# A decoder step on one core: expert turns of the second half reassigned between four stages, and the first weight blocks of three stages loaded one stage ahead

## The reference

```python
n1 = rms_norm(x, norm1_w) * (1 + sc1) + sh1
h = n1 @ w_in                                    # 8704 columns
oa = hgrn(h) ; ob = merge of 3 window attentions # softmax-weighted by head
mix = sigmoid(gA) * (oa @ w_branch_a) + sigmoid(gB) * (ob @ w_branch_b)
x = x + g1 * (mix @ w_out)
n2 = rms_norm(x, norm2_w) * (1 + sc2) + sh2
q = rms_norm((n2 @ wq).reshape(T, 8, 256), qn_w)
s1, s2 = q[..., :128] @ k1, q[..., 128:] @ k2    # top 16 of each, then 16 of 256 pairs
x = x + g2 * sum over 8 heads x 16 picks of  softmax(sc) * gelu(n2 . u[e]) * v[e]
```

## The kernel before

| stage of the second half | before | after |
|---|---|---|
| norm 1, project, hgrn | 130 | 130 |
| attention | 26 | 27 |
| merge | 34 | 14 |
| branch | 4 | 7 |
| out | 4 | 8 |
| norm 2 | 6 | 6 |
| query | 14 | 26 |
| rest (alone) | from 242 | from 242 |

## Time and profile before

### The profile page before, as it was taken

One profiled execution on the slowest core, in us unless ns is written; L12 is line 12 of the kernel. 1 busy time (PEld: TensorE's weight loads), 2 busy tenths in 40 slices (PEclk: granted clock), 3 DMA queues, 4 the chain that ended last, 5 costly groups with the idle time before them and its releaser, 6 DMA issues. The chain is left out here.

```text
span 4682.4 us, 46850 instructions
## 1 busy us (share of the span) xinstructions
PE 3284.7 (70%) x14275; PEld 1729.4 (37%) x14275; DVE 2604.3 (56%) x6546; ACT 1943.4 (42%) x6689; POOL 1482.3 (32%) x1167
## 2 busy tenths in 40 slices
PE   4998878764997899776664478796555555555556
PEld 2777665641543335444442145472111111111111
DVE  2171532366545565386556643536767767667674
ACT  1122330145445644464543321434545545545554
POOL 2553100253322223222223210213444444444443
PEclk7998789887998999876887789897777777777779
DMA  5534244388988889876898995758999999999998
GB/s 207 214 131 147 67 134 146 122 322 341 383 329 299 304 322 382 311 265 239 342 351 341 419 363 184 255 192 325 425 413 426 426 411 421 420 407 422 420 414 340
DMA packets 311887, 1449.31 MB, mean 310 GB/s; under 512 B 41042, under 2 KB 102386, under 8 KB 163283
## 3 DMA queue, kind: packets, MB, share of 16 engines
q0 software_dynamic: 152064, 1107.36, 58.8%
q1 hardware_dynamic: 145202, 331.75, 20.2%
q10 hardware_dynamic: 14368, 7.21, 0.5%
HBM read 1378.82 MB, written 74.57 MB: 310 GB/s over the span
## 5 line engine op out<-in xcount | busy, mean ns | idle before, releaser
L2408 POOL DMA_INDIRECT uv_ring<-in_peer_uv,pick_idx x1024 | 1169.3, 1142 | 2394.8 <-PE expert_acc L2573 1999.5
L2573 PE MATMUL expert_acc<-uv_ring,diag 128*64 128x512 f32 x3968 | 1281.5, 782 | 738.7 <-ACT diag L2543 708.0
L2500 DVE SCALAR_TENSOR_TENSOR uv_ring<-uv_ring,n_pairs 128x1024 f32<-128x1024 f32 x1024 | 1245.2, 1231 | 690.2 <-DMA uv_ring<-in_peer_uv,pick_idx 609.7
L2573 PEld LDWEIGHTS expert_acc<-uv_ring,diag 128*64 128x64 f32 x3968 | 294.9, 165 | 1622.6 <-ACT diag L2543 1112.5
L2530 ACT ACTIVATE gelu_cube<-dots_now 128x2 f32<-128x2 f32 x528 | 106.0, 201 | 947.8 <-DVE uv_ring L2500 916.8
L2538 ACT ACTIVATE pick_weight<-gelu_tanh,pick_share 128x1 f32<-128x1 f32 x1056 | 350.9, 379 | 17.7
L2543 ACT ACTIVATE diag<-half_pattern,pick_weight 128x64 f32<-128x64 f32 x1024 | 300.4, 340 | 16.5
L692 PE MATMUL h_acc_q<-in_w_all_q,n_all_q 128*128 128x512 f32 x640 | 288.3, 604 | 0.0
L2533 ACT ACTIVATE gelu_tanh<-gelu_cube,dots_now 128x1 f32<-128x1 f32 x1056 | 253.2, 286 | 16.2
L2535 ACT ACTIVATE pick_share<-dots_now,pick_prob 128x1 f32<-128x1 f32 x1056 | 245.2, 279 | 0.0
L689 PE MATMUL h_acc_q<-n_all_q,in_w_all_q 128*128 128x272 f32 x896 | 219.2, 401 | 10.1 <-DMA in_w_all_q<-in_w_in 10.1
(11 more groups left out here) (440 smaller groups left out, 4830.8 us busy)
## 6 DMA issues: line engine op xcount, KB each, us to landing
in_w_p<-in_w_in SPq DMA_DIRECT2D x34, 1024.0 KB, 7.2
in_w_all_q<-in_w_in SPq DMA_DIRECT2D x17, 2048.0 KB
ada_w<-in_w_ada SPq DMA_DIRECT2D x12, 2048.0 KB, 8.0
uv_ring<-in_peer_uv,pick_idx POOLq DMA_INDIRECT x1024, 14.7
past_keys_q<-in_past_keys SPq DMA_DIRECT2D x16, 1024.0 KB, 10.1
past_rows_q<-in_past_values SPq DMA_DIRECT2D x16, 1024.0 KB, 10.3
score_pair<-scores SPq DMA_DIRECT2D x66, 128.0 KB, 7.0
wq_raw_p<-in_peer_wq SPq DMA_DIRECT2D x16, 512.0 KB
```

Of the source, the lines that this page charges most:

```text
L2408: pool.indirect_dma_start(self.rows_of(part, s), None, self.x["peer_uv"][0], bass.IndirectOffsetOnAxis(ap=self.idx[:, q % 2, s, k:k + 1], ...
L2500: ins = dve.scalar_tensor_tensor(out=row, in0=row, scalar=1.0, in1=self.n2[:, tile % 2, s if tile < LAST_TILE else 0, :], op0=ALU.mult, op ...
L2573: ins = pe.matmul(self.acc[s * 64:(s + 1) * 64, c, :], self.diag[:, part % DIAGS, s, :], rows, start=first, stop=last)
```

## The change

The COST values are raised in branch, out and query of the second half and lowered in merge, `FRONT_US` goes from 2010 to 2003, and the turns move as the table above says. The tiles and semaphores of the first weight blocks become objects (`BranchWeights`, `OutWeights`, `PeerWeights`) that are allocated a stage earlier, and their `first()` is issued by SP in the stage in front: branch blocks 0 and 1 at the start of merge in the first half (in the second half still in branch, but ahead of the gates), out blocks 0 and 1 (1 MB each) in branch after its first loads in both halves, and query's keys, key weights and blocks 0 and 1 in norm 2 in both halves. Later blocks are loaded as before.

```diff
+class BranchWeights:
+    def load(self, m):
+        for j, name in enumerate(("w_branch_a", "w_branch_b")):
+            self.nc.sync.dma_start(self.w[:, m % 2, j], self.x[name][m]).then_inc(self.landed[m % 2], 16)
+    def first(self):
+        self.load(0)
+        self.load(1)
...
+class OutWeights:
+    def load(self, q):
+        self.nc.sync.dma_start(self.w[:, q % 2], self.w_out[q]).then_inc(self.landed[q % 2], 16)
...
+class PeerWeights:
+    def first(self):
+        self.load_keys(0)
+        with self.nc.allow_non_contiguous_dma("a weight for each column"):
+            self.nc.sync.dma_start(self.key_w[:], self.x["peer_qn_w"].rearrange("a (j p) -> p (a j)", p=P)).then_inc(self.key_w_in, 16)
+        self.load(0)
+        self.load(1)
...
 def norm_phase(...):
+        if peer_weights is not None:
+            peer_weights.first()
         for n, w, at in tiles:
...
 def merge_phase(...):
-    COST, COST_S = 12.0, 40.0
+    COST, COST_S = 5.2, 17.0
...
+        if branch_weights is not None:
+            branch_weights.first()
         beside.gap("sp", 2)
...
 def branch_phase(...):
-    COST = 2 * HEADS * 2 * sum(max(0.11, k * 0.00042) for _, k in pieces)
+    COST = 3.6 * HEADS * 2 * sum(max(0.11, k * 0.00042) for _, k in pieces)
...
-            at_least(sp, y_done, 2 * (m - 1))
-            for j, name in enumerate(("w_branch_a", "w_branch_b")):
-                sp.dma_start(w[:, s, j], x[name][m]).then_inc(w_in[s], 16)
+            if m > 1:
+                sp.wait_ge(y_done, 2 * (m - 1))
+                weights.load(m)
...
+        if span.samples:
+            weights.first()
         load(0)
         load(1)
+        out_weights.first()
...
 def out_phase(...):
-    COST = DC * 2 * max(0.11, PART * 0.00042)
+    COST = DC * 3.6 * max(0.11, PART * 0.00042)
...
-        load(0)
         for n, w, at in tiles:
             sp.dma_start(x1[0:w, n, :], src_rows(at, w)).then_inc(rows_in, 16)
...
-        load(1)
         next_gains.load()
...
 def query_phase(...):
-    C_Q = (3 if span.split else 3.7) * DC * sum(max(0.11, k * 0.00046) for _, k in pieces)
-    C_S = 0.8
+    C_Q = (3 if span.split else 7.0) * DC * sum(max(0.11, k * 0.00046) for _, k in pieces)
+    C_S = 1.5
...
-            if u < UNITS:
+            if 1 < u < UNITS:
...
-        load_w(0)
-        if span.split:
-            load_w(1)
-        load_keys(0)
-        with nc.allow_non_contiguous_dma("a weight for each column"):
-            sp.dma_start(key_w[:], x["peer_qn_w"].rearrange("a (j p) -> p (a j)", p=P)).then_inc(key_w_in, 16)
...
-FRONT_US = 2010.0
+FRONT_US = 2003.0
```

More of the change, by code:

```diff
@@ new lines, with __init__, load, load_keys @@
+class OutWeights:
+    def __init__(self, nc, keep, tag, x):
+        self.nc, self.w_out = nc, x["w_out"]
+        self.w = keep("w_out" + tag, [P, 2, DC, 2 * P])
+        self.landed = [nc.alloc_semaphore(name="w_out0_in" + tag), nc.alloc_semaphore(name="w_out1_in" + tag)]
+    def load(self, q):
[4 more added lines that the diff above has]
+class PeerWeights:
+    def __init__(self, nc, keep, tag, x):
+        self.nc, self.x = nc, x
+        self.raw, self.keys, self.key_w = keep("wq_raw" + tag, [P, 2, DC, P]), keep("peer_keys" + tag, [P, 2, 2, P]), keep("peer_key_w" + tag, [P, 2])
+        sem = lambda name: nc.alloc_semaphore(name=name + tag)
+        self.raw_in, self.keys_in, self.key_w_in = [sem("wq0_in"), sem("wq1_in")], [sem("peer_keys0_in"), sem("peer_keys1_in")], sem("peer_key_w_in")
+    def load(self, u):
+        self.nc.sync.dma_start(self.raw[:, u % 2], self.x["peer_wq"][u]).then_inc(self.raw_in[u % 2], 16)
+    def load_keys(self, h):
+        for j, name in enumerate(("peer_k1", "peer_k2")):
+            self.nc.sync.dma_start(self.keys[:, h % 2, j, :], self.x[name][0, h]).then_inc(self.keys_in[h % 2], 16)
+    def first(self):
+        self.load_keys(0)
+        with self.nc.allow_non_contiguous_dma("a weight for each column"):
+            self.nc.sync.dma_start(self.key_w[:], self.x["peer_qn_w"].rearrange("a (j p) -> p (a j)", p=P)).then_inc(self.key_w_in, 16)
+        self.load(0)
+        self.load(1)
@@ L280, in norm_phase @@
+def norm_phase(nc, ph, span, beside, const, gains, loaded_here, n_hi, n_lo, src_rows, held, keep_rows, peer_weights=None):
     sb, psum, sem = ph.sb, ph.psum, ph.sem
@@ L1445, in attention_constants, with merge_phase @@
     return out
-def merge_phase(nc, ph, span, beside, const, past_values, consts, dram, q_s, s_rows, o_b):
+def merge_phase(nc, ph, span, beside, const, past_values, consts, dram, q_s, s_rows, o_b, branch_weights):
     sb, psum, sem = ph.sb, ph.psum, ph.sem
@@ L1690, in _, with branch_phase @@
             nc.tensor.transpose(p_turned[:, 0:P], o_rows[:], ident[:]).then_inc(o_turned, 1)
-def branch_phase(nc, ph, span, beside, const, x, dram, o_a, o_b, mix, new_kv_p, new_kv_s):
+def branch_phase(nc, ph, span, beside, const, x, dram, o_a, o_b, mix, new_kv_p, new_kv_s, weights, out_weights):
     sb, psum, sem = ph.sb, ph.psum, ph.sem
@@ L1698, in branch_phase @@
     NP = len(pieces)
[L1699 removed]
+    w, w_in = weights.w, weights.landed
     gates = sb("branch_gates", [P, 2, 2, T])
@@ L1785, in _, with out_phase @@
             beside.pe(COST)
-def out_phase(nc, ph, span, beside, const, x, dram, src_rows, mix, x1, next_gains):
+def out_phase(nc, ph, span, beside, const, x, dram, src_rows, mix, x1, next_gains, weights):
     sb, psum, sem = ph.sb, ph.psum, ph.sem
@@ L1794, in out_phase @@
     N_PARTS = D // PART
-    w_o = sb("w_out", [P, 2, DC, PART])
+    w_o, w_in = weights.w, weights.landed
     gate_p = sb("gate1_p", [P, D])
@@ L1811, in load @@
                 return
-            at_least(sp, out_done, (q - 1) * N)
-            sp.dma_start(w_o[:, q % 2], x["w_out"][q]).then_inc(w_in[q % 2], 16)
-        load(0)
+            sp.wait_ge(out_done, (q - 1) * N)
+            weights.load(q)
         for n, w, at in tiles:
@@ L1872, in _, with query_phase @@
                 beside.pe(COST)
-def query_phase(nc, ph, span, beside, const, x, dram, n_hi, n_lo, next_gains):
+def query_phase(nc, ph, span, beside, const, x, dram, n_hi, n_lo, next_gains, weights):
     sb, psum, sem = ph.sb, ph.psum, ph.sem
@@ L1885, in query_phase @@
     SLOTS = 2
-    raw = sb("wq_raw", [P, 2, DC, P])
+    raw, keys, key_w = weights.raw, weights.keys, weights.key_w
+    raw_in, keys_in, key_w_in = weights.raw_in, weights.keys_in, weights.key_w_in
     if span.split:
@@ L1940, in load_keys @@
                 at_least(sp, key_turned, h - 1)
-                for j, name in enumerate(("peer_k1", "peer_k2")):
-                    sp.dma_start(keys[:, h % 2, j, :], x[name][0, h]).then_inc(keys_in[h % 2], 16)
+                weights.load_keys(h)
         def query(h, j):
@@ L2751, in front @@
                         n_hi, n_lo = both(last, "n2", "right")
+                        peer_weights = PeerWeights(nc, lambda name, shape: held_as(last, name, shape, "right"), tag, x)
                     with ExitStack() as rows:
@@ L2755, in front @@
                                       tag + "2", span, x["norm2_w"], dram["mod"], 3 * D, 4 * D)
-                        phase(out_phase, tag, busy, span, beside, const, x, dram, x_rows, mix, x1, gains)
+                        phase(out_phase, tag, busy, span, beside, const, x, dram, x_rows, mix, x1, gains, out_weights)
                         late.close()
@@ L2759, in front @@
                             n_hi, n_lo = both(last, "n2")
-                        phase(norm_phase, tag + "2", busy, span, beside, const, gains, False, n_hi, n_lo, None, x1, n2_rows)
-                    phase(query_phase, tag, True, span, opening() if opening else beside, const, x, dram, n_hi, n_lo, coming)
+                            peer_weights = PeerWeights(nc, lambda name, shape: held_as(last, name, shape, "left"), tag, x)
+                        phase(norm_phase, tag + "2", busy, span, beside, const, gains, False, n_hi, n_lo, None, x1, n2_rows, peer_weights)
+                    phase(query_phase, tag, True, span, opening() if opening else beside, const, x, dram, n_hi, n_lo, coming, peer_weights)
             return coming
```

34 lines of the change are left out of this document (21 added, 13 removed).

## The result

The changed kernel took 4628.4 us (median of 4 runs, 4622.9 to 4640.3) beside 4684.9 us before on the same chip: a ratio of 0.9872, 95% interval 0.9853 to 0.989. Measured once more later, in five runs, it took 4623.6 beside 4696.1 us, 0.9857 (0.9836 to 0.9878). The forecast was 4633, range 4590 to 4670. The profiled execution has a span of 4627.1 us.

A forecast was written before the change was run, and what follows sets the result against it. Transfers were taken to bound merge, attention and rest, while PE bound query, out and branch, with transfer time unused. Terms -100 + 7 + 30 + 14 + 6 + 1 - 12 = -54 us gave 4633 us, range 4590 to 4670.

The forecast's parts named there:

- Merge, -100: Second half's merge: 34 turns become 14, 44.6 MB leave at 425 GB/s, 105 us less 5 us idle; bounds -113 to -65.
- 145 to 160 us: Sign for the merge: this time with a DMA share above 0.85 would confirm the largest term.
- rival 1: Merge becomes bound by landing time of past values in three slots: 190 us instead of 153, whole 4670 us; chance 0.10.
- Attention, +7: Second half's attention gets one part and turn 180's loads of 1 MB at a share of 0.94: +7 us.
- Query, +30: Second half's query: 12 more parts, 24.6 us on PE, 9.6 DVE delay, -4 from the preload; bounds +20 and +45.
- rival 2: Query and branch: PE waits for each turn's `diag`, a moved part costs about 8.3 us, whole 4743 us; chance 0.05.
- Branch, +14: Second half's branch: 22 us of added transfers push the end set by ACT's blocked issue, less 8 us idle; bounds +6, +24.
- Out, +6: Second half's out: 4 more parts, 8.2 us on PE, less 2.4 us for the moved 1 MB; bounds 0 and +12.
- Norm 2, +1: Second half's norm 2: same turns, 1.2 MB more at a share of 0.87 under DVE and ACT; bounds 0 and +3.
- First half, -12: First half's branch, out and query: first weight blocks are there at the barrier, -12 us together; bounds -13 and -4.
- rival 4: Five shorter stage starts keep PE at 2.4 GHz: 5 x 1.65 = 8 us, up to 4 more in query; 4621 us, 0.06.
- Rest, 0: Parts from turn 242 on stay at 5.23 us each, 1485 us; growth would mean turns were delayed, not moved.

The follow-up runs named there:

- keys_first: Changed kernel with the merge's sample keys, mask and new values issued ahead of the six att_parts loads: 4614.4 us, 0.9831, merge 158.6 us.
- two_slots: Changed kernel with two buffers for past values instead of three: 4644.0 us, 0.9895, merge 178.2 us.
- preload_only: Changed kernel with the old costs (merge 34 parts, branch 4, out 4, query 14), so only the first loads are moved: 4675.8 us, 0.998.
- turns_only: Kernel before with the new costs alone (merge 14 parts, branch 7, out 8, query 26), every first load where it was: 4648.9 us, 0.9911.
- half_dose: Changed kernel with half of the turns moved (merge 24 parts, branch 5, out 6, query 20): 4633.8 us, 0.9873.
- keys_early_half: Changed kernel with half the turns moved, cache copies on SP, sample keys loaded during attention, mask and new values ahead of att_parts: 4618.5 us, 0.9844.

## Why the prediction was right, and where its steps were not

**Merge, -100, measured -81 and -86.** The mechanism was right: a stage at a share of 0.95 gave back what its gathers cost. But the merge lies outside the 145 to 160 us that I named as a sign. Mis-sized were two things. The transfers that left are 96.83 - 55.34 = 41.5 MB and not 44.6, 97.6 us at 425 GB/s and not 105: the gathers in the stage fell by 71.28 - 31.91 = 39.4 MB, not 42.6. My 2.13 MB a part came from a window that began 3 us ahead of the barrier. And by my estimate the 28 gathers that are left (128 rows of 8 KB each) make 29.4 of the 31.91 MB, so that the rest was in flight from attention. And the idle time rose from 0.05 x 250 = 13 to 0.15 x 169 = 25 us, where I had allowed 5. I wrote that the start "stays"; it grew by 6 to 7 us, from keys at 16.1 us behind the barrier to 22.0 and 23.0.

The traces of all runs say more on this. With 34 parts in the merge the keys come at 16.1 and 16.5 us, with 24 at 20.7, with 14 at 22.0 to 23.4 (six profiles), with 5 at 18.2. What sets the first two apart from all others is turn 180: its four loads of n2, 1 MB, are issued 6 to 10 us into the merge there, behind the keys, and 7 to 19 us ahead of the barrier in the others, in front of them. I had charged this megabyte to attention alone. That it makes the keys late fits, but was not tested by itself.

That the start is one of the places is shown by keys_first, whose earlier keys made the merge shorter. The waits for past values, 4.0 to 29.0 us, are the rest; two_slots shows them to be worth something, and I had put them all into rival 1. That rival's figure, 190 us, added chains end to end that in fact overlap.

**Attention, +7, measured 0 to +2.** Not decided. Over the profiles of this study attention took 264 to 282 us, and 276.4 in preload_only, whose turns are those of before. What I sized is smaller than what the stage varies by.

**Query, +30, measured +26 and +28, by other steps.** Against preload_only, the 12 parts cost 35 to 37 us, about my 24.6 + 9.6; the moved loads bring 8.5, not 4. My lower bound was also added up wrongly: 24.6 with all 8.7 gone is +16, not +20. PE's waits in the changed kernel's query:

```profile
PE expert_acc L2626 <- ACT diag L2596: 11.0, 5, 3.0
PE peer_scores_q L2095 <- DVE score_stage_q L2132: 7.6, 6, 3.2
PE peer_keys_turned_q L2064 <- PEq L2728: 1.9, 1, 1.9
```

The 9.6 us for later score units did not come: that wait fell from 11.2 to 7.6 us. In their place stands rival 2's wait for `diag`, 11.0 us where I had 0. Rival 2 had the right mechanism and a wrong size, a few us on five turns and not 6 us on each; by the table of doses its price of 5.5 us a part is not reached even at 55 parts, though 4.4 comes near. PE was busy 221.55 us against the 228 expected, at a granted clock of 0.95 where it was 0.92.

**Branch, +14, measured +3 and +6.** The end of this stage is ACT's blocked issue, as I said. The longest four copies took 13.75 us in the first profile and 19.43 in the second, against 16.18, and all 30 together 55.1 and 60.2 against 49.7; the stretch without transfers shrank from 22 to 13 us, and to pieces of at most 6 us in the second. So the signs that I named came, but I charged every added transfer in full to that end. The stage also started sooner. The first matmuls of before and of the changed kernel (start us, us):

```profile
2746.15 5.99 PE L1782 MATMUL branch_acc_q<-o_a_q,branch_w_q 128*128 128x272 f32 x16 [11.19 <-DMA branch_w_q<-in_w_branch_b]
```

```profile
2642.24 5.83 PE L1846 MATMUL branch_acc_q<-o_a_q,branch_w_q 128*128 128x272 f32 x16 [4.63 <-DMA branch_w_q<-in_w_branch_b]
```

They come 10.0 and 3.5 us after the barrier. In turns_only it is 3.4 us, in preload_only 10.2 us. So it is the turns and not the loads. I had written "so that wait stays". It doesn't go down evenly with the dose: half_dose and keys_early_half, with 24 parts, have 10.0 and 10.4 us. In these, in before and in preload_only four or more gathers were issued in the merge's last 14 us; in all kernels with 3.4 to 4.0 us it was two or none. That the first weights then find shorter queues is my reading of this; no run moved these gathers alone. The gain of 6.5 us is most of what the branch's sum lacked.

My reading of the Trainium skill, DMA: Bandwidth & Descriptors, Queues, rings and completion order, under which parts and preloads here would cost 22 us, was not borne out by the stage's time. That reading also went beyond the page: its turns between queue rows let a load of SP's row go beside gathers that wait in another, so it doesn't say that a preload overtakes none. No run here shows the order of packets itself.

**Out, +6, measured +6 and +8.** As written: no wait for `w_out`, PE's first matmul at the barrier, then DVE's first unit late instead (DVE waits 19.4 us for the gate rows, 20.2 before), though PE's own wait for it was 4.0 us and not 5 or more. But the 2.4 us that I took off for the moved megabyte did not come: turns_only, with the old loads, also has 98.2 us. PE's earlier start did not make the stage end sooner. **Norm 2, +1, measured -2**: its 1.2 MB more cost nothing under DVE and ACT.

**First half, -12, measured -15 and -18**, of which -13.3 and -15.7 in branch, out and query and the rest in stages that were not changed. PE's first matmul of branch and out is at the barrier, against the earlier trace rows:

```profile
705.99 1.28 ACT L1816 ACT_TABLE_LOAD   x1 [2.90 <-PEq L2728]
...
706.02 5.37 PE L1846 MATMUL branch_acc_p<-o_a_p,branch_w_p 128*128 128x512 f32 x8 [3.12 <-PEq L2728]
```

The same eight matmuls took 5.37 us instead of 6.16. That is rival 4 in small, 0.8 us at a start for which I had priced 1.65. It is the clock: over these matmuls (711 to 717.2 us before, 706 to 711.4 after) the granted clock is 0.60 and 0.68, and 6.16 x 0.60 and 5.37 x 0.68 are both 3.7 us. Five such starts would be 4 us, an estimate; only this one was read.

**Rest, 0, measured +9 and -1.** The longer rest of the first profile is scatter: other kernels with the same 284 parts gave 1486 to 1497 us. The frame held: turns were moved, not put off. The median of 4628 was hit within 5 us, partly by luck, since a merge term 17 us too large met a branch term 10 us too large and a first half, norm 2 and hgrn better than forecast. The range has a slip of its own: everything in favour of merge, query and branch by my bounds is 4633 - 13 - 10 - 8 = 4602 us, and "near 4590" takes rival 4's 12 us as well.

## What to carry to other kernels

Work that is moved out of a stage bound by transfers is worth its transfers there only as long as something else keeps the queues full; look for the stage's own starting chain before counting on all of it, and read its waits from the barrier on, since part of such a wait can lie in front of it. The price at the receiver is not constant: here it went from about 2 to over 4 us a part, so try half the dose first, and expect a flat optimum. DMA issues on an engine that also computes hold its compute; give them to a queue on which nothing waits.

## What the runs showed of the hardware

- The issue of four cache copies took from 2.7 to 13.75 us on ACT's queue within one stage, up to 19.43 us in the second profile of the same kernel, and up to 12.88 us on SP's. The issue itself can be slow, whichever of the two engines does it. Taken off ACT with nothing else changed, it left a branch of 96 us in place of 105 and 108.
- A load of 192 KB was with PE 11.3 us after its issue even as the first issue of its stage (keys_first), and 18.9 us after it with six loads of 260 KB in front (the changed kernel). The share was nine tenths or more for nearly all that time: gathers and loads that were already under way were still moving.
- With nearly the same instructions (26 or 27 turns), attention took from 264 to 282 us in different profiles, mostly by PE's waits for `k_raw` (28 to 49 us), while the rest took 1486 to 1497. A term of under 10 us in such a stage can't be read from one profile each.
